# Two seams of the delta-rule layer: gate logit weights split in the stage before, first heads' blocks stored apart

## The reference, cut to what matters

```python
h = rms_norm(x, pre_norm_w[0])
proj = h @ w_in                       # q, k, v, z and two logits per value head
qkv, z, b_logit, a_logit = split(proj)
qkv = silu(causal_depthwise_conv(qkv, conv_w))
q, k, v = split(qkv)                  # 8 key heads, 16 value heads of 128
beta = sigmoid(b_logit)
g = -exp(A_log) * softplus(a_logit + dt_bias)
# per head, in 8 chunks of 64 tokens:
a_mat = strict_lower((k*beta) @ k.T * decay)
u, w = solve(I + a_mat, v*beta), solve(I + a_mat, k*beta*exp(g))
# and over the chunks a state S:
v_new = u - w @ S;  o = q_dec @ S + qk @ v_new;  S = S*decay_end + k_dec.T @ v_new
y = (rms_norm(o) * silu(z)) @ w_out
```

## Time and profile before

| | us |
|---|---|
| median of 3 runs | 3066.44 |
| lowest and highest | 3062.43, 3069.53 |
| the profiled execution: its own time | 3068.61 |
| its span | 3066.8 |
| PE busy in it | 2833.7 (92%) |
| DVE, ACT, POOL busy | 1836.6, 1205.0, 661.1 |

### The profile page before, as it was taken

One profiled execution on the slowest core, in us unless ns is written; L12 is line 12 of the kernel. 1 busy time (PEld: TensorE's weight loads), 2 busy tenths in 40 slices (PEclk: granted clock), 3 DMA queues, 4 the chain that ended last, 5 costly groups with the idle time before them and its releaser, 6 DMA issues. The chain is left out here.

```text
span 3066.8 us, 39238 instructions
## 1 busy us (share of the span) xinstructions
PE 2833.7 (92%) x14634; PEld 2443.7 (80%) x14634; DVE 1836.6 (60%) x3338; ACT 1205.0 (39%) x2120; POOL 661.1 (22%) x401
## 2 busy tenths in 40 slices
PE   7989789999989999999999999799969979999998
PEld 6879458779889999998788888688757757788877
DVE  4434543359997888666788887635924544344442
ACT  3433552232326766432333333367434433222221
POOL 0012110003332333365232322043022320000000
PEclk9999899999999999999999999899989989999999
DMA  3201112333436888999999999567365431322222
GB/s 125 83 30 56 50 53 85 137 135 126 141 113 235 287 315 301 332 382 383 356 361 354 361 358 353 181 183 219 117 199 159 141 120 63 110 96 96 96 103 69
DMA packets 251468, 572.34 MB, mean 187 GB/s; under 512 B 43616, under 2 KB 152032, under 8 KB 222272
## 3 DMA queue, kind: packets, MB, share of 16 engines
q1 hardware_dynamic: 212160, 426.56, 41.5%
q0 software_dynamic: 36864, 134.23, 11.2%
q10 hardware_dynamic: 2304, 9.70, 0.9%
HBM read 486.38 MB, written 84.02 MB: 186 GB/s over the span
## 5 line engine op out<-in xcount | busy, mean ns | idle before, releaser
L42 PE MATMUL pe_ps<-hh,pe_uh 128*128 128x384 f32 x1024 | 351.3, 343 | 19.6 <-issue 16.8
L44 PE MATMUL pe_ps<-hh,pe_ul 128*128 128x384 f32 x1024 | 345.2, 337 | 0.0
L43 PE MATMUL pe_ps<-hl,pe_uh 128*128 128x384 f32 x1024 | 345.1, 337 | 0.0
L42 PE MATMUL pe_ps<-pe_vh,pe_whi 128*128 128x512 f32 x768 | 299.5, 390 | 3.4 <-DVE pe_vl L1647 3.4
L43 PE MATMUL pe_ps<-pe_vl,pe_whi 128*128 128x512 f32 x768 | 299.5, 390 | 0.0
L44 PE MATMUL pe_ps<-pe_vh,pe_wlo 128*128 128x512 f32 x768 | 299.4, 390 | 0.0
L1476 POOL DMA_INDIRECT pe_gu<-in_u_rows,pe_urow x128 | 199.3, 1557 | 309.3 <-DVE pe_gu L1608 283.3
L1484 POOL DMA_INDIRECT pe_gv<-in_v_w,pe_vrow x128 | 156.5, 1223 | 332.3 <-DVE pe_acc L1617 318.5
L42 PEld LDWEIGHTS pe_ps<-hh,pe_uh 128*128 128x128 f32 x1024 | 194.9, 190 | 21.9 <-issue 21.6
L1608 DVE SCALAR_TENSOR_TENSOR pe_gu<-pe_gu,pe_xs 128x1024 f32<-128x1024 f32 x128 | 155.1, 1220 | 88.7 <-DMA pe_gu<-in_u_rows,pe_urow 88.4
L43 PEld LDWEIGHTS pe_ps<-hl,pe_uh 128*128 128x128 f32 x1024 | 195.0, 190 | 0.3
(11 more groups left out here) (589 smaller groups left out, 6985.8 us busy)
## 6 DMA issues: line engine op xcount, KB each, us to landing
xu<-in_u_w SPq DMA_DIRECT2D x64, 1024.0 KB
pe_v_raw<-in_v_w SPq DMA_DIRECT2D x64, 1024.0 KB, 8.3
hidden_scratch<-pe_hs SPq DMA_DIRECT2D x64, 384.0 KB
gate_scratch<-pe_stage SPq DMA_DIRECT2D x24, 1024.0 KB, 10.9
pe_hw<-hidden_scratch SPq DMA_DIRECT2D x64, 384.0 KB
pe_gate<-gate_scratch SPq DMA_DIRECT2D x64, 384.0 KB
gf_raw<-in_gdn_w SPq DMA_DIRECT2D x16, 1024.0 KB, 7.2
gb_pk<-pk_scratch SPq DMA_DIRECT2D x64, 256.0 KB, 2.8
```

Of the source, the lines that this page charges most:

```text
L42: pe.matmul(out, lh, rh, start=start, stop=False)
L43: pe.matmul(out, lh, rl, start=False, stop=False)
L44: return pe.matmul(out, ll, rh, start=False, stop=stop)
```

## The change

It has two parts. (1) A class `GfFirst` puts the logit weights, their two halves and `raw[0]` at fixed places. The expert stage loads the logit weights right after the gelu of the gathered dots, and head 0's weights when step 62 is split; ACT makes the high part after its last split, DVE the low part after the first add to `x`. The buffers of the expert stage's last part are laid out anew so that these places are free. The front stage loses both loads, the split and the wait on `ba_lo`. (2) In step 14 SP loads the z weights first; then it stores the blocks of heads 0 and 1 alone, four DMAs of 16 partitions, and loads them after the store of `keep_v(5)`. The blocks of heads 2 to 7 are stored from the back stage, four DMAs of 48 partitions, ahead of `load_z(2)`; behind it SP waits for them and for the last two value stores, before the loop. The first 12 matmuls of the z projection (4 of 8 k of f = 0) move to the end of the front stage, and the four `next(ahead)` of step 0 go. The tiles `area` and `vb` now lie where `ot` will be, PSUM is shared by the two stages, and ACT waits for the stores before it first writes `ot`.

```diff
@@ peer: SP
                 sp.wait_ge(act_ok, 1)
+                sp.dma_start(nxt.ba[:], nxt.ba_dram).then_inc(nxt.ba_in, 16)
                 sp.dma_start(gain[:], gain_dram.partition_broadcast(P)).then_inc(gain_in, 16)
+                sp.wait_ge(v_lo, NU - 1)
+                sp.dma_start(nxt.raw[:], nxt.w_dram).then_inc(nxt.raw_in, 16)
@@ peer: ACT, after the last low_v
+                act.wait_ge(nxt.ba_in, 16)
+                act.wait_ge(wv_lo, NU - 1)
+                act.activation(nxt.bah[:], nxt.ba[:], ACT.Copy).then_inc(nxt.ba_hi, 1)
@@ peer: DVE, after the add to x of L1670
+                dve.wait_ge(nxt.ba_hi, 1)
+                dve.wait_ge(outp, NU - 1)
+                dve.tensor_tensor(nxt.bal[:], nxt.ba[:], nxt.bah[:].bitcast(F32), ALU.subtract).then_inc(nxt.ba_lo, 1)
@@ gdn_front: SP
-                sp.dma_start(flat(raw[0][:])[:, 0:KD * P].rearrange("p (k c) -> p k c", k=KD), ba_dram).then_inc(ba_in, 16)
...
-                sp.wait_ge(ba_lo, 1)
-                sp.dma_start(raw[0][:], source(0)).then_inc(w_in[0], 16)
...
+                    if it == KH + 6:
+                        low_done(sp, NB - 2)
+                        sp.dma_start(first_z.raw[:], first_z.src).then_inc(first_z.raw_in, 16)
+                        sp.wait_ge(elim, 2 * (H - 1))
+                        sp.wait_ge(turned_u, 1)
+                        sp.wait_ge(kept_u, 1)
+                        sp.wait_ge(cleared, 1)
+                        for a in range(2):
+                            store_blocks(sp, rc_dram, flat(at), a, slice(0, 2), rc_out)
+                        for a in range(2):
+                            store_blocks(sp, ud_dram, utf, a, slice(0, 2), u_out)
                     if it > KH:
                         keep_v(it - KH - 1)
                     if it == KH + 6:
-                        sp.wait_ge(elim, 2 * (H - 1))
-                        sp.dma_start(ud_dram.rearrange("a h i c t -> (a h i) (c t)"), utf).then_inc(u_out, 16)
...
-                        sp.dma_start(rc_dram.rearrange("a h i c t -> (a h i) (c t)"), flat(at)).then_inc(u_out, 16)
-                low_done(sp, NB - 2)
-                sp.dma_start(first_z.raw[:], first_z.src).then_inc(first_z.raw_in, 16)
...
+                        sp.wait_ge(first.zeroed, 4)
+                        sp.wait_ge(rc_out, 32)
+                        load_first(rc_dram, first.rc, first.rc_in)
+                        sp.wait_ge(u_out, 32)
+                        load_first(ud_dram, first.ub, first.ub_in)
                 keep_v(KH - 1)
                 for b in range(2):
-                    sp.wait_ge(vb_out[b], 16 * (KH // 2))
+                    sp.wait_ge(vb_out[b], 16 * (KH // 2 - 1))
@@ gdn_front: ACT
-                act.wait_ge(ba_in, 16)
-                act.activation(flat(bah[:]), flat(raw[0][:])[:, 0:KD * P], ACT.Copy).then_inc(ba_hi, 1)
...
+                high(0)
                 act.wait_ge(small_in, 16 * 3)
                 act.activation(small[LO, 2:3], small[LO, 0:1], ACT.Exp).then_inc(row_a, 1)
-                high(0)
                 high(1)
@@ gdn_front: DVE
-                dve.wait_ge(ba_hi, 1)
-                dve.tensor_tensor(flat(bal[:]), flat(raw[0][:])[:, 0:KD * P], flat(bah[:]).bitcast(F32), ALU.subtract).then_inc(ba_lo, 1)
@@ gdn_front: PE, at the end
+                pe.wait_ge(first_z.w_hi, 1)
+                pe.wait_ge(first_z.w_lo, 1)
+                pe.wait_ge(vb_ok, KH - 1)
+                for k in range(GDN_Z0):
+                    mm3(pe, ps[:, GDN_BZ, :], (first_z.wh[:, k, :], first_z.wl[:, k, :]), (hh[:, k, :], hl[:, k, :]), k == 0, False)
@@ gdn_back: SP
                     load_at(l, B)
+                for a in range(2):
+                    store_blocks(sp, rc_dram, first.at, a, slice(2, KH), first.rest_out)
+                    store_blocks(sp, ud_dram, first.ut, a, slice(2, KH), first.rest_out)
                 load_z(2)
+                sp.wait_ge(first.kept, 32)
+                sp.wait_ge(first.rest_out, 16 * 4)
                 for g in range(LAST):
@@ gdn_back: PE, at all four places of a step
-                    next(ahead, None)
                     if g:
+                        next(ahead, None)
```

More of the change, by code:

```diff
@@ L1111, in _, with peer @@
                     turn(NT - 1)
-def peer(nc, hh, hl, x, ident, drams, g_dram, h_dram, load, store, first_q):
+def peer(nc, hh, hl, x, ident, drams, g_dram, h_dram, load, store, first_q, nxt):
     pq_dram, keys_dram, iota_dram, u_dram, v_dram, urows_dram, gain_dram = drams
@@ L1789, in _, with store_blocks, gdn_front @@
                     last.then_inc(back, 1)
-GDN_F = 640
+GDN_F, GDN_BZ, GDN_Z0 = 640, 5, 4
 GDN_QK, GDN_KD, GDN_VB, GDN_AT = (slice(a, b) for a, b in ((0, 256), (256, 384), (384, 512), (512, 640)))
-def gdn_front(nc, hh, hl, ident, gcols, rows_dram, sd_dram, ad_dram, ud_dram, rc_dram, pk_dram, drams, first, first_z):
-    w_dram, ba_dram, conv_dram, alog_dram, dt_dram, reset_dram, mask_dram = drams
+def store_blocks(sp, dram, tile, a, heads, signal):
+    rows = slice((a * GDN_KH + heads.start) * NCH, (a * GDN_KH + heads.stop) * NCH)
+    sp.dma_start(dram[a, heads].rearrange("h i c t -> (h i) (c t)"), tile[rows, :]).then_inc(signal, 16)
+def gdn_front(nc, ps, hh, hl, ident, gcols, rows_dram, sd_dram, ad_dram, ud_dram, rc_dram, pk_dram, drams, first_w, first, first_z, ot_end):
+    w_dram, conv_dram, alog_dram, dt_dram, reset_dram, mask_dram = drams
     KH, NB, H = GDN_KH, 2 * GDN_KH, C // 2
@@ L1803, in gdn_front @@
         wl = [nc.alloc_sbuf_tensor_at(f"gf_wl{u}", weights, F32R, offset=at0[u] + 8 * 1024) for u in range(2)]
-        raw = [nc.alloc_sbuf_tensor_at(f"gf_raw{u}", weights, F32, offset=at0[u] + 16 * 1024) for u in range(2)]
-        bah, bal = (ph.sb(n, [P, KD, P], F32R) for n in ("bah", "bal"))
+        raw = [first_w.raw, nc.alloc_sbuf_tensor_at("gf_raw1", weights, F32, offset=at0[1] + 16 * 1024)]
+        bah, bal, ba_hi, ba_lo = first_w.bah, first_w.bal, first_w.ba_hi, first_w.ba_lo
+        area = ph.sb("area", [P, 2 * C * C + 1536])
+        vb = [ph.sb(f"vb{u}", [P, NCH, P]) for u in range(2)]
+        assert nc.sbuf_base <= ot_end
         conv = ph.sb("conv", [P, KH, 4, 4])
@@ L1886, in share @@
             return mine
+        first.at, first.ut = flat(at), utf
         with nc.Block() as block:
@@ L1928, in keep_v, with load_first @@
                     sp.wait_ge(vb_ok, m + 1)
-                    sp.dma_start(packed(m, GDN_VB), vb[m % 2][:]).then_inc(vb_out[m % 2], 16)
+                    sp.dma_start(packed(m, GDN_VB), vb[m % 2][:]).then_inc(vb_out[m % 2] if m < KH - 2 else first.kept, 16)
+                def load_first(dram, tiles, signals):
+                    for l in range(2):
+                        for a in range(2):
+                            half = slice(a * C, (a + 1) * C)
+                            sp.dma_start(tiles[l][half, :, half], dram[a, l, 0:4].rearrange("i c t -> c i t")).then_inc(signals[l], 16)
                 for it in range(NB):
@@ L2570, in _ @@
                     if c and i in (5, 7):
+                        if c == 1 and i == 5:
+                            act.wait_ge(first.rest_out, 16 * 4)
+                            act.wait_ge(first.kept, 32)
                         finish(i // 7, c - 1)
@@ L2801, in _ @@
                     carry(1, g)
-                    next(ahead, None)
+                    if g:
+                        next(ahead, None)
                     spread(0, g)
```

88 lines of the change are left out of this document (50 added, 38 removed).

## The result

The changed kernel is slower: 3076.68 us median (3075.92 to 3081.07, 8 runs) against 3066.61 us for the kernel before (3062.43 to 3069.53, 8 runs), a ratio of 1.0037 with a 95% interval of 1.0028 to 1.0046. That is 10.1 us more where 4.8 less was forecast, and outside the range. The profiled execution took 3076.44 us with a span of 3074.7, 7.9 more than the span of before.

What follows compares the result with a forecast made beforehand. PE, busy for 92% of the span, was taken as the bound, so only its waits or needless work could give time. 7.2 + 8.3 - 10.7 = 4.8 us less: 3061.6 us against the median of 3066.44, range 3050 to 3072.

Steps and rivals of the forecast that it cites:

- I cost all this at nothing: Expert stage: two added loads, an ACT copy, a DVE subtraction and their waits would cost 0 us.
- The cover of 1.5: Expert stage's end: 1.5 us of cover left; a longer delay would go one for one into the stage's end.
- D: Rival, chance 0.08: added loads or subtraction exceed the expert stage's cover, or head 0's weights come late; 3 us off, 3064.6.
- C: Rival, chance 0.09: store time follows bytes per partition everywhere, first four stores too; back stage starts 1.4 us later; 3076.5.
- First seam, 7.2 us: Front stage: logits start at the barrier's end, so the row operations start 7.2 us sooner; gain 7.2 us.
- Second seam, 8.3 us: Before the back stage: PE is last, not SP, and the back stage starts 8.3 us sooner.
- Back stage, 10.7 us: Back stage's first steps: corner(4) waits behind the stores of heads 2 to 7, then PE's clock is lower; loss 10.7 us.
- R: Back stage: time the four stores of heads 2 to 7 take to flow, taken as 15.7 us, between 7.9 and 21.0.
- Time follows the bytes of a partition: Back stage, upper end for the four stores of heads 2 to 7: 5.24 us each, 21.0 us together.
- Rival B: Chance 0.14: rows of one store crowd on a few paths, the four back-stage stores take 21.0 us; no change, 3066.9.
- the 16 to 19 given as a sign: Back stage: SP would wait some 16 to 19 us on the stores of heads 2 to 7.
- A: Rival, chance 0.27: the back-stage stores flow at 400 GB/s in 7.9 us; gain 14.6 us, 3051.8.

Runs made afterwards that it cites:

- experiment 7: Kernel before plus only the change's part 1, its tiles 128 bytes lower so that offsets are equal: ratio 0.9972 (0.9961 to 0.9983) to the kernel before.
- experiment 1: Kernel before with only the new places of the expert stage's last buffers: 3072.88 us against 3064.55 for the kernel before.
- experiment 6: Kernel before plus only the change's part 2, with the old places and logit weights handled as before: 3073.57 us against 3064.55.
- experiment 2: The whole change with the upper buffer group and the two logit halves 128 bytes lower, making offsets equal: 3065.77 us, one run.
- experiment 11: Whole change, offsets equal, no rest stores; rc and ud each stored in the first stage as two DMAs of 64 partitions: 3058.21 us, ratio 0.9979.
- experiment 8: Whole change, offsets equal, no rest stores; rc and ud each stored whole by one 128-partition DMA in the first stage: 3047.91 us median, ratio 0.9944.

## Why the prediction was wrong

**The expert stage: the step that failed.** "I cost all this at nothing" held for what it counted, the two loads, the copy and the subtraction (cover 1.55 us left; experiment 7 shows no loss). The cover of 1.5 is worked out from the 1950.80 of the earlier trace rows: less 2.8 us for the last step's 12 matmuls, 0.23 us apart in the kernel before, it is 1948.0, and the subtraction of 1.2 us then ends at 1949.3. What was not counted is the rest of part 1, the new places of the buffers. The description of the change had them, and they have no instruction, so they got no term and stood at nothing without a reason. The runs showed 2304 matmuls slowed from 226.7 to 232.0 ns apart, because stationary and moving tiles had come to stand 128 bytes apart. That cost 11 us of loop in experiment 1 and 12.3 in the change: most of the 14.9 us between the forecast's 4.8 less and the 10.1 more that was measured. None of the rivals had it: D priced delays at the loop's end, and C reached 3076.5 by another way, one that did not happen.

**First seam, 7.2 us: right.** 7.2 between the same two events in experiment 7, 6.7 in the change, whose copy is 0.46 us longer. That it fits to 0.1 is part luck. The row chain, from which the 7.2 was taken, starts 6.5 us sooner after the last `pe_vl` split in experiment 7 and 6.1 in the change, in part because PE ran 12 matmuls of the logits 0.43 us apart, at a granted clock of 0.50, and not 9 (8.2 us from the first's start to the last's end, not the 7.65 of before).

**Second seam, 8.3 us: right.** 8.1 in the change, 8.2 in experiment 6, and for the reason given: PE is last, not SP. The paces of 0.44 and 0.23 us, with which its 12 z matmuls were counted, are those of the logits in the kernel before; in the change the granted clock from 2232.97 to 2237.00 was 0.50. Counted from the copy's end, SP was done after 15.4 us (worked out: 15.9) and PE after 17.1 (16.6).

**Back stage, 10.7 us: right in kind, the term R mis-sized.** The chain came as written: wait for the rest stores, pk loads first, then rc, PE idle for 13 us and then at a granted clock of 0.50 until 2285.5, 5.3 us where 3.98 was taken over. R was taken as 15.7, half the rate of whole stores, an estimate that no row of before showed. By the prediction's own terms (flow from T+15.0, landing 1.4 after it) the landing at T+35.5 makes it 19.1, outside the 13 to 18 of the forecast. "Time follows the bytes of a partition" gave 21.0, nearer than half the rate. Rival B had 0.14 where it should have led, because I let half the rate stand for stores of 48 rows. The 19.1 is not clean: the four stores landed at 2261.5, 2266.0, 2269.7 and 2275.8, and `load_z(2)`, 512 KB that SP issued at 2262.85 and that landed at 2277.4, was in flight beside the last one. The sum had no term for it, and what it added to the 19.1 is open. SP's own wait was 10.2 us and not the 16 to 19 given as a sign, since issuing the last two stores and the z load kept it until 2265.6. With R = 19.1 the prediction's formula loses 14.1; 13.4 was measured.

**The sum.** With 12.3 for the loop and 13.4 for the back stage the terms are 12.3 - 7.2 - 8.3 + 13.4 = +10.2, and 10.1 was measured between the medians. That close a match is luck: the two profiled spans differ by 7.9. Without the loop it would have been -2.1, no change; the one run of experiment 2 took 1.2 more than its neighbour, within the scatter of single runs.

**The rivals.** A (fast stores) fell: no store over part of the partitions ran near 400 GB/s (the windows of experiment 11 show 244 and 182 with 48 rows and 215 with 64, other transfers included). B was nearest for the stores, 21.0 against 19.1; that their rows crowd on a few paths was a guess, and no run shows it. C's condition for the small stores was not met: `rc` landed within 6 us of its issue, and SP sent the loads of `ud` at 2232.6 without a wait, well ahead of the 2243.0 at which C had it land. D's cause did not occur: DVE kept 1.55 us of cover, and head 0's split was ready before the logits ended.

## What to carry to other kernels

When a change moves buffers, treat the operands of each matmul as part of the change. Keep stationary and moving tiles at equal offsets: 0 and 256 bytes apart ran at 226.6 to 226.9 ns from start to start here, while 32, 64 and 128 bytes cost 2.5 to 3%. Which offset they shared did not matter (443 matmuls in 100 us at 768 and at 896 within 1 KB), nor that one buffer's set stood apart from the other's (443 too). Compare the mean duration of the matmul groups of both traces before looking for waits.

In a place like this one, store a tile whole over its 128 partitions rather than the part that is needed first. Here 4 MB landed within 11.4 us. The part that was wanted sooner landed 2 us (`rc`) and 5 us (`ud`) sooner after its issue, by the medians above, which the back stage's start did not show (18.2 against 18.5 us), and the rest, sent later, cost 13 us behind a wait at the head of the load queue.

## What the runs showed of the hardware that was not expected

- At a granted clock of 1.00 with PE never idle, a 128x512 fp32r matmul with its weight load took 1/443 of 100 us with equal offsets, and 1/430 to 1/432 with its operands 32, 64 or 128 bytes apart (2.5 to 3% slower). At 256 bytes apart it was as fast as at equal offsets (226.9 ns from start to start in project(0) and project(1)). A matmul whose own operands agreed was slow too when the weights loaded next stood 128 bytes off (232.1 ns). Why is open.
- Stores from 64 of the partitions kept the DMA engines as busy as whole ones while they moved half the bytes (215 against 419 GB/s, DMA share 0.97 and 1.02), so the busy share of DMA did not show the loss, only the GB/s did.
- SP issued the two whole stores of experiment 8 in 0.33 (`rc`) and 0.43 us (`ud`); the four small ones of the change took it 0.79 us for the two of `rc` and 3.78 for the two of `ud`.
